# A gated recurrence whose projections are split into two fp32r parts, with all heads' values and output gates computed first

## What is computed

```python
u_x = rms_norm(h_lat, norm_mix_w[l]) * (1.0 + sc1[:, None]) + sh1[:, None]
px = jnp.split(u_x @ w_in_l, split_pts, axis=-1)      # pc likewise from the context

def hg_dir(p, z, lb):
    q = jax.nn.silu(to_heads(p[4], HG_HEADS))
    f = lbh + (1.0 - lbh) * jax.nn.sigmoid(to_heads(z, HG_HEADS))
    return q, 1.0 - f, to_heads(p[7], HG_HEADS), jnp.log(f)   # queries, keys, values, logs

# per chunk, with b = cumsum(log f):
scores = einsum('bhtsd,bhsd->bhts', qc[:, :, :, None, :] * decay, kc)
out = scores @ vc + (qc * exp(b)) @ state
new_state = exp(b_end) * state + (kc * exp(b_end - b)).T @ vc

b = from_heads(rms_norm(o_hg, hg_norm_w_l)) * jax.nn.silu(p[8])   # output gate p[8]
```

## Time and profile before

| | |
|---|---|
| median of the runs | 2821.18 us |
| profiled execution, its own time | 2818.32 us |
| its span | 2816.7 us |
| granted TensorE clock, mean | 0.978 |
| PE busy | 2651.4 us, 94% |
| DVE busy | 2079.2 us, 74% |
| ACT busy | 1426.4 us, 51% |
| POOL busy | 543.3 us, 19% |

### The profile page before, as it was taken

How to read it: one execution, slowest core, us unless ns; L and a number is a source line. 1 busy time by engine, 2 the same in 40 slices (tenths; PEclk the granted TensorE clock), 3 DMA queues, 4 the chain that set the end, 5 groups by cost and what they waited for, 6 DMA issues and landing times. The chain is left out here.

```text
span 2816.7 us, 43469 instructions
## 1 busy us (share of the span) xinstructions
PE 2651.4 (94%) x15273; PEld 2208.2 (78%) x15274; DVE 2079.2 (74%) x2433; ACT 1426.4 (51%) x1442; POOL 543.3 (19%) x437
## 2 busy tenths in 40 slices
PE   7899999899798899999999999999999999999994
PEld 3668577577687779777887978899989897888783
DVE  4566676673666796999879787866686778967884
ACT  4433535331634574777647565544454546645653
POOL 0524434200013211222121111111121112111110
PEclk9999999999899899999999999999999999999997
DMA  7101100180353796999969787866586769967864
GB/s 260 31 23 31 30 24 16 49 289 1 118 137 124 289 381 218 367 354 351 320 221 363 259 294 262 283 203 205 192 293 207 256 235 329 326 207 272 300 227 134
DMA packets 266663, 596.96 MB, mean 212 GB/s; under 512 B 21373, under 2 KB 47141, under 8 KB 265473
## 3 DMA queue, kind: packets, MB, share of 16 engines
q1 hardware_dynamic: 246208, 552.82, 54.9%
q0 software_dynamic: 20384, 43.19, 6.9%
HBM read 578.01 MB, written 42.25 MB: 220 GB/s over the span
## 5 line engine op out<-in xcount | busy, mean ns | idle before, releaser
L2100 ACT ACTIVATE whi<-e_slot 128x2048 fp32r<-128x2048 f32 x296 | 560.9, 1912 | 437.2 <-PE e_acc L2026 370.8
L2162 DVE TENSOR_TENSOR e_slot_r<-e_slot,whi 128x2048 fp32r<-128x2048 f32 x296 | 674.9, 2287 | 101.1 <-ACT whi L2100 101.1
L2023 PE MATMUL e_acc<-e_xhi,whi 128*128 128x256 f32 x1664 | 399.4, 282 | 3.2 <-ACT e_xhi L2104 3.2
L2100 ACT ACTIVATE whi<-slot 128x2048 fp32r<-128x2048 f32 x148 | 283.3, 1914 | 192.1 <-PE e_acc L1998 192.1
L2162 DVE TENSOR_TENSOR slot_r<-slot,whi 128x2048 fp32r<-128x2048 f32 x151 | 344.7, 2285 | 19.7 <-ACT whi L2100 16.7
L1996 PE MATMUL e_acc<-whi,e_ahi 128*128 128x512 f32 x800 | 319.4, 399 | 0.0
L2023 PEld LDWEIGHTS e_acc<-e_xhi,whi 128*128 128x128 f32 x1664 | 313.1, 188 | 6.3 <-ACT e_xhi L2104 6.3
L1940 POOL DMA_INDIRECT sum<-yo,e_idx_now x50 | 122.3, 2446 | 1012.3 <-issue 539.4
L1998 PE MATMUL e_acc<-whi,e_alo 128*128 128x512 f32 x800 | 313.4, 392 | 0.0
L1997 PE MATMUL e_acc<-e_slot_r,e_ahi 128*128 128x512 f32 x800 | 311.6, 389 | 0.0
L1996 PE MATMUL e_acc<-whi,e_xhi 128*128 128x512 f32 x768 | 303.3, 395 | 0.8 <-DVE e_slot_r L2162 0.5
(11 more groups left out here) (338 smaller groups left out, 4794.8 us busy)
## 6 DMA issues: line engine op xcount, KB each, us to landing
e_slot<-in_w SPq DMA_DIRECT2D x296, 1024.0 KB, 7.1
slot<-in_w SPq DMA_DIRECT2D x151, 1024.0 KB, 7.3
rv<-in_w_ada SPq DMA_DIRECT2D x32, 512.0 KB, 4.7
slot<-in_w_in SPq DMA_DIRECT2D x20, 512.0 KB, 4.1
wa<-in_w_ada SPq DMA_DIRECT2D x8, 1024.0 KB, 17.1
slot<-in_w_in SPq DMA_DIRECT2D x6, 1024.0 KB, 8.6
xt<-in_x SPq DMA_DIRECT2D x8, 512.0 KB, 14.7
slot<-in_w_out SPq DMA_DIRECT2D x4, 1024.0 KB, 13.0
```

The source lines that it names most:

```text
L2023: pe.matmul(out[:, c, :], whi[i % RING][:, w], xhi[:, kk, :], start=first, stop=False, skip_group_check=True)
L2100: act.activation(whi[i % RING][:], raw[i % PIECES][:], ACT.Copy).then_inc(S["whi_made"], 1)
L2162: v.tensor_tensor(wlo[i % PIECES][:], raw[i % PIECES][:], whi[i % RING][:].bitcast(F32), ALU.subtract).then_inc(S["wlo_made"], 1)
```

## The change

All projections of `hgrn2` are computed in split form. Rows are split once at the stage's start and the two parts are kept (`uhi`, and `uT_r` over `uT`) for this stage and the next. Values of all heads come first, then keys and queries of head 0, then the output gates of all heads in two pairs of heads; both go out to DRAM and come back one head at a time. Keys, logs and queries have one buffer each. The two products that finish an output gate move from VectorE to GpSimd, over 1024 columns.

```diff
+        key = [over(f"h_key{d}", d) for d in range(2)]
+        cum = [over(f"h_cum{d}", 2 + d) for d in range(2)]
...
+            def turned_products(h, i, chunk, a, z):
...
+                pe.wait_ge(S["cw_low"], c + 1)
...
                 for k in range(KT):
+                    pe.matmul(out, hi[:, k, :], uhi[:, k, a:z], start=(k == 0), stop=False)
+                    pe.matmul(out, lo[:, k, :], uhi[:, k, a:z], start=False, stop=False)
+                    mm = pe.matmul(out, hi[:, k, :], ulo[:, k, a:z], start=False, stop=(k == KT - 1))
...
+            values(0, (0, 1))
+            values(1, (0, 1))
+            values(0, (2,))
+            values(1, (2,))
+            for x in range(2, NT):
+                values(x, (0, 1, 2))
+            for i in range(6):
+                gates_of_keys(0, i)
+            queries(0, 0)
+            queries(0, 1)
+            for x in range(6):
+                output_gates(x)
+            turn_keys(0, 0)
+            turn_keys(0, 1)
+            for n in range(2, 6):
+                output_gates(4 + n)
+                turn_keys(0, n)
+            output_gates(10)
+            output_gates(11)
+            updates(0)
+            for x in range(12, 2 * LT):
+                output_gates(x)
+            for h in range(HEADS):
+                more = h + 1 < HEADS
+                for j in range(HT):
+                    scores(h, j)
+                    if j:
+                        output(h, j - 1)
                 if more:
+                    gates_of_keys(h + 1, 0)
                 else:
                     early_rows(0)
+                output(h, HT - 1)
+                if more:
+                    for i in range(1, 4):
+                        gates_of_keys(h + 1, i)
...
+                for j in range(HT, LT):
+                    scores(h, j)
+                    if j > HT:
+                        output(h, j - 1)
+                    if more and j < HT + 2:
+                        gates_of_keys(h + 1, 4 + j - HT)
                 if more:
                     queries(h + 1, 0)
...
@@ scalar @@
+            def copy_z(h, i):
+                d, j = z_order(h)[i]
...
+                if h:
+                    act.wait_ge(S["lev_ready"], 2 * h - (j < 2))
...
             def logs(h):
+                act.wait_ge(S["z_copied"], 6 * h + 6)
...
+            def high_chunk(n):
+                act.wait_ge(w_in[n % 2], 16 * (n // 2 + 1))
+                act.activation(Whi[n % 2], W[n % 2], ACT.Copy).then_inc(S["cw_high"], 1)
@@ gpsimd @@
+            def gates(h):
+                g.wait_ge(S["g_sig"], h + 1)
+                g.tensor_tensor(gate_row, kdec[1][:, 0:SEQ], gate_row, ALU.mult).then_inc(S["gate_part"], 1)
+                g.wait_ge(S["gate_part"], h + 1)
+                g.tensor_tensor(gate, gate, nw[:].unsqueeze(1).to_broadcast((P, LT, P)), ALU.mult).then_inc(S["gate_ready"], 1)
@@ vector @@
+            def low_chunk(n):
+                v.wait_ge(S["cw_high"], n + 1)
+                v.tensor_tensor(Wlo[n % 2], W[n % 2], Whi[n % 2].bitcast(F32), ALU.subtract).then_inc(S["cw_low"], 1)
...
                 if now:
-                    for j in range(HT):
+                    pick(h, 0)
+                    if more:
+                        low_chunk(3 * h + 3)
+                        low_chunk(3 * h + 4)
+                    else:
+                        low_early(0)
+                        low_early(1)
+                    for j in range(1, HT):
                         pick(h, j)
...
                 if more:
                     cumulate(h + 1, 1)
+                    if now:
+                        low_chunk(3 * h + 5)
```

More of the change, by code:

```diff
@@ L577, in output @@
                 mm.then_inc(S["o_done"], 1)
-            for h in range(-1, HEADS):
-                now, more = h >= 0, h + 1 < HEADS
-                if now:
-                    for j in range(HT):
-                        scores(h, j)
-                        if j:
-                            output(h, j - 1)
+            values(0, (0, 1))
[4 more added lines that the diff above has]
+                values(x, (0, 1, 2))
@@ L586, in _ @@
+            for h in range(HEADS):
+                more = h + 1 < HEADS
[3 more added lines that the diff above has]
+                        output(h, j - 1)
                 if more:
-                    gates_of_keys(h + 1, 0, 0)
+                    gates_of_keys(h + 1, 0)
                 else:
                     early_rows(0)
-                if now:
-                    output(h, HT - 1)
-                if not more:
+                output(h, HT - 1)
+                if more:
+                    for i in range(1, 4):
+                        gates_of_keys(h + 1, i)
+                else:
@@ L707, in _ @@
+            for i in range(6):
+                copy_z(0, i)
+                if i == 4:
+                    high_chunk(2)
             act.wait_ge(S["eps_set"], 1)
             act.wait_ge(S["bounds"], 3)
-            for h in range(-1, HEADS):
-                now, more = h >= 0, h + 1 < HEADS
+            logs(0)
+            query_sig(0, 0)
+            query_sig(0, 1)
+            key_decays(0)
+            output_gate(0)
+            output_gate(1)
+            query_decays(0)
+            output_gate(2)
@@ new lines, in _ @@
+            output_gate(3)
+            high_gates(1)
+            output_gate(4)
+            output_gate(5)
+            turned_keys(0, 0)
+            turned_keys(0, 1)
+            for n in range(2, 6):
+                output_gate(4 + n)
+                turned_keys(0, n)
+                levels(0, 0, (n - 2,))
+            for x in range(10, 2 * LT):
+                output_gate(x)
+                if x < 12:
+                    levels(0, 0, ((4,), (5, 6))[x - 10])
+            high_chunk(3)
@@ L711, in _ @@
+            high_chunk(4)
+            gate_sig(0)
+            for h in range(HEADS):
+                more = h + 1 < HEADS
+                if h and more:
+                    high_chunk(3 * h + 3)
+                    high_chunk(3 * h + 4)
+                if not more:
+                    high_early(0)
+                    high_early(1)
                 if more:
                     copy_z(h + 1, 0)
-                if now:
-                    roots(h, 0)
-                    levels(h, 1, range(0, 2))
+                roots(h, 0)
+                levels(h, 1, range(0, 2))
@@ L735, in _ @@
-                if now:
-                    roots(h, 1)
+                levels(h, 1, range(4, 6))
+                if more:
+                    copy_z(h + 1, 3)
+                levels(h, 1, range(6, NL))
+                if more:
+                    copy_z(h + 1, 4)
+                    copy_z(h + 1, 5)
+                    logs(h + 1)
+                    high_chunk(3 * h + 5)
+                    query_sig(h + 1, 0)
+                else:
+                    for x in range(3):
+                        early_rows(x)
@@ L737, in _ @@
+                roots(h, 1)
                 if not more:
@@ L785, in _ @@
                     levels(h + 1, 0)
+                    gates(h + 1)
         @block.vector
```

551 lines of the change are left out of this document (326 added, 225 removed).

## The result

| | before | after |
|---|---|---|
| median, same chip (4 runs each) | 2820.68 us (2819.34 to 2823.1) | 2908.8 us (2905.78 to 2911.04) |
| ratio, 95% interval | | 1.031 (1.029 to 1.033) |
| profiled execution, its span | 2818.32, 2816.7 us | 2906.67, 2905.0 us |
| granted TensorE clock | 0.978 | 0.951 |

The account below looks back on a forecast made before the run. The prediction took a chain of about 107 us through POOL, VectorE and others, under TensorE's 116, to bound the heads once TensorE's work left. Front +63.5, three heads +17, last head 0 gave +80.5: 2901.7 us, range 2857 to 2930.

Parts of the forecast that it names:

- The bound: In a head before the change, TensorE's 116 us cover a chain of about 107 us through the other engines, by 9 us.
- TensorE's work sets the length of a head: Rival for the heads: TensorE's work decides, heads take 74 us, total falls by 69 us to 2752; chance 0.10.
- The front: Ahead of head 0's first score: values and gates of all heads move there, 63.5 us longer, bounds 58 to 72.
- a wait for the second bank: Ahead of head 0's scores: the second gate tile waits for PSUM until 24.9 us after head 0's key groups end.
- The head: Heads 0 to 2, first score to first score: 121 us each instead of 116.2, bounds 113 to 128; three add 17.
- score 4 to the sixth group (E): In each head on TensorE: score 4, a key group, score 5, an output and the last key group, 15.6 us.
- clock, three pauses: In each head: slow products after pauses before the first score, score 4 and queries cost 2 us each, bounds 0 and 2.5.
- The last head: From head 3's first score to the next stage's first product: 64.6 us against 64.5, so no change.
- The signs: Expected profile after: first score near 215 us, heads 118 to 124 apart, PE busy near 70, 8 us idle before score 4.
- A looser chain: Rival for the heads: POOL's subtractions take 16.5 us instead of 23.8, no clock loss, total +43, 2864; chance 0.17.
- A tighter one: Rival: blocked low parts, POOL's gate operations and queued gate stores add 5 us a head, 9 in front, 2926; chance 0.11.
- The rule against the chain: In the heads: two-SBUF-input VectorE and GpSimd operations exclude each other for one whole instruction; a head up to 3 us longer.

## Why the prediction was right

*The bound.* The step on which all rests, that a chain of about 107 us lies beneath a TensorE of 116, is shown by leaving work out before the change (107 to 110 us), and the rival "TensorE's work sets the length of a head" falls by that run and by leaving out 25.5 us after it.

*The front.* Values ended at 109.8 us (forecast 110), the first gate tile started at 157.36 after 9.1 us of idle (157.2, 9), the first score at 215.6 (214.9). The term was right, with a little luck in its parts: the first gate tile stood behind that pause and took 5.9 us instead of 2.84, which no term had; 2.3 of these 3.1 us took the place of a wait for the second bank (E+22.6 to E+24.9) that the forecast had and that did not come. Where TensorE has less to do there, the chain of levels and states holds the first score at 202 us.

*The head.* Term by term, head 2 against the forecast:

| | forecast | measured | pauses filled (head 1) |
|---|---|---|---|
| first score to POOL's levels | 12.8 | 15.5 | 12.5 |
| levels until ready | 25.9 | 26.0 | 26.0 |
| idle before score 4 | 8 | 7.9 | |
| score 4 to the sixth group (E) | 15.6 | 18.0 | 15.7 |
| E to POOL's levels of the next head | 25.3 | 27.2 | 25.1 |
| these levels | 23.8 | 24.6 | 24.7 |
| VectorE's tail, then states | 5.0 + 7.2 | 3.8 + 7.9 | 3.8 + 7.2 |
| clock, three pauses | 6 | (in the rows above: 2.7 + 2.4 + 1.9) | |
| sum | 121 | 123.1 | 115.0 |

With the pauses filled, every term but POOL's second stream and VectorE's tail lies within 0.3 us of its forecast, and the sum without a clock term, 115.7, was measured as 115.0: this shows the chain itself. The mis-sized term is the clock: 7.0 us against 6 in three rows, 0.7 more in the states, whose last updates ran slowly too, and 7.4 to 8.0 by the run with filled pauses. POOL's second stream brings 0.8 more, the tail 1.2 less. (The idle 8 us lie within the levels' row and are no term of the sum.) Over three heads it is 369.0 us against 364. The forecast's own terms, 115.7 and three times 2, add up to 121.7 a head, not 121: 366 for three.

Head 0 reached its 123.5 us by other terms. No pause stood ahead of its first score (2.0 us), but its low parts came later, because ScalarE's copies of the next weights waited for their load; POOL's levels started 16.7 us behind the first score, and the first pick, released by a gate store, started 0.4 us behind its score, where the forecast had 1 us for the stores. The copy:

```profile
221.38 1.06 ACT L762 ACTIVATE slot_r<-slot 128x1024 fp32r<-128x1024 f32 x1 [5.19 <-DMA slot<-in_w_in]
```

*The last head* was +2.2 instead of 0. The terms of the forecast do not give its 64.6 us: 64.5 + 4.5 + 2 - 1.5 - 7.3 is 62.2. Two of them failed. The low parts of the early weights were right (4.49 us between the first two picks), but the clock cost 3.6 us instead of 2: POOL's levels started 18.7 us behind the first score (17 by my terms), because that score and score 3 were slow:

```profile
598.01 0.80 PE L685 MATMUL h_po<-h_val,h_st 128*128 128x128 f32 x2 [3.82 <-DVE h_st L1097]
...
651.32 0.53 PE L1266 MATMUL p_pb<-h_early,uhi 128*128 128x512 f32 x1 [2.65 <-PEq L372]
```

And of the 7.3 us of idle ahead of the next stage 2.65 remained, so the part behind score 4 became 6.0 us shorter, not 8.8. The slip in this sum (2.4 too much) and that in the heads (2.2 too little) cancel in the forecast of +80.5, which is luck.

*The signs.* Met: first score near 215, distances within 118 to 124, 8 us ahead of score 4 released by `h_wq`, pauses before `h_po` and the queries, 3.5 us before each first score released by `h_state`, clock below 0.95, groups of 5.6 us. Missed: PE busy near 70 us a head; it showed 78 to 82, since products at the lower clock count longer (about 70 by the run with filled pauses). No gate store held TensorE.

*The other rivals.* "TensorE's work" would have shown heads of 74 us. "A looser chain" wanted POOL at 16.5 us in the first half of a head's levels; it stayed at 24.6. "A tighter one" named low parts blocked behind POOL and GpSimd's gate operations running into the levels: the two low parts ran in 2.35 us while POOL was idle, so nothing could block them, and the gate operations ended before the levels.

*The rule against the chain.* The sum of keys took 8.12 us beside seven pairs of POOL's subtractions at 1.2 to 1.4 us, so VectorE was held far longer than one instruction. By the Trainium skill, SBUF — State Buffer, SBUF: two separate sides, whichever starts first keeps the ports "for the whole instruction". The sum's 8.12 us do not agree with that, since it waited through those seven pairs. The low part of the query weights does: it started just ahead of a POOL operation, which took 3.82 to 3.83 us in heads 1 to 3, where before the change, with no low part there, it took 2.90 (the first row is of the kernel before):

```profile
443.81 2.90 POOL L760 TENSOR_TENSOR h_cum<-h_ktok,h_cum 128x1280 f32<-128x1280 f32 x1 [2.83 <-DVE h_ktok L797]
...
536.42 1.20 DVE L1014 TENSOR_TENSOR slot_r<-slot,slot_r 128x1024 fp32r<-128x1024 f32 x1
536.59 3.83 POOL L956 TENSOR_TENSOR h_cum<-h_ktok,h_cum 128x1280 f32<-128x1280 f32 x1 [2.87 <-DVE h_ktok L1030]
```

The first two low parts ran beside an idle POOL and do not bear on it. The 0.9 us cost no time, as POOL waits 6.05 us for TensorE right behind (`h_po`).

## What to carry to other kernels

An engine that is 94% busy can be 9 us away from a chain that no busy share shows: add up, from one landing to the next, the waits of the others before you take work off it or move the work that hides them. When a buffer is made single, look for where its producer stands in the stream; here moving two groups into a pause gave back half of the loss, since two PSUM banks could hold what the buffer could not. And count what the first products behind each new pause cost at the lower clock.

## What the hardware showed that I had not expected

A VectorE operation with two SBUF inputs that arrives while POOL's subtractions follow one another closely waited until POOL's stream was over, 8.1 to 8.5 us in heads 0 to 2; issued 2.5 us behind the stream's start it took 1.0 us, and from then on both took turns (POOL 1.8 us a pair instead of 1.2). It is not only how far the stream has come: in the run with work taken off TensorE the same sum, each time 8.0 us behind the stream's start, took 0.7 us in heads 0 and 1 and 9.0 in head 2. What decides it was not settled.

Short pauses of TensorE were followed by slow products. In the kernel before, behind 3.3 us of waiting after steady work, a score took 3.7 us instead of 2.0; after the change, behind 3.5 us of waiting, two took 3.7 and 3.0, but there a pause of 9.5 us and slow updates had come just ahead. The length of the last pause alone does not tell: behind 1.8 us each time, with work taken off TensorE before the change, the first scores took 2.1, 3.7 and 2.6 us.
